# Two gated feed-forward blocks of a Trainium2 kernel: 18 of 22 gate/up pairs of each as seven block products instead of eight

## What is computed

```python
def second_block(x, ..., norm2_g, w_gate, w_up, w_down, final_g):
    for l in range(2):
        ...
        h = rms_norm(x, norm2_g[l])
        x = x + (jax.nn.silu(h @ w_gate[l]) * (h @ w_up[l])) @ w_down[l]
    return rms_norm(x, final_g)
```

## Time and profile before

| what | us |
|---|---|
| median of 3 runs (lowest to highest) | 2635.52 (2634.99 to 2636.14) |
| span of the profiled execution, first to last instruction | 2634.2 |
| what lies around the span: median less span | 1.3 |
| TensorE busy (share) | 2619.0 (99%) |
| VectorE busy (share) | 1418.1 (54%) |
| ScalarE busy (share) | 1010.3 (38%) |
| GpSimd busy (share) | 110.9 (4%) |
| mean granted TensorE clock | 0.998 of full speed |

### The profile page before, as it was taken

How to read it: one execution, slowest core, us unless ns; L and a number is a source line. 1 busy time by engine, 2 the same in 40 slices (tenths; PEclk the granted TensorE clock), 3 DMA queues, 4 the chain that set the end, 5 groups by cost and what they waited for, 6 DMA issues and landing times.

```text
span 2634.2 us, 33330 instructions
## 1 busy us (share of the span) xinstructions
PE 2619.0 (99%) x13877; PEld 2134.3 (81%) x13877; DVE 1418.1 (54%) x2209; ACT 1010.3 (38%) x1484; POOL 110.9 (4%) x87
## 2 busy tenths in 40 slices
...
GB/s 403 132 190 209 271 195 195 80 96 81 81 70 76 81 81 65 96 99 99 98 90 118 80 64 64 107 98 92 96 98 126 80 65 54 106 91 109 96 93 76
DMA packets 46744, 296.55 MB, mean 113 GB/s; under 512 B 5121, under 2 KB 7297, under 8 KB 17410
## 3 DMA queue, kind: packets, MB, share of 16 engines
...
q10 hardware_dynamic: 2, 0.00, 0.0%
...
## 4 chain that ended last, share of the span: by engine, by line
PE 96%; ACT 1%; DVE 1%; DMA 1%; issue 0%; SPq 0%; DVEq 0%; ACTq 0%
PE PS L565 95%; PE PS L623 1%; ACT WH L1078 0%; DMA RAW<-stream 0%; DMA AR<-stream 0%; DVE AA L1553 0%; DVE XT L1553 0%; ACT TMP L1078 0%; ACT AA L1078 0%; DVE Tb L1553 0%; ACT H1H L1078 0%; DVE WL L1553 0%; DVE AR L1576 0%; DVE SPL L1556 0%; DVE Vb L1826 0%
## 5 line engine op out<-in xcount | busy, mean ns | idle before, releaser
L565 PE MATMUL PS<-H1H,WH 128*128 128x512 f32 (+1 forms) x2144 | 826.6, 386 | 0.4 <-DVE H1L L1553 0.3
L565 PE MATMUL PS<-H1H,WL 128*128 128x512 f32 (+1 forms) x2144 | 814.5, 380 | 0.0
L565 PE MATMUL PS<-H1L,WH 128*128 128x512 f32 (+1 forms) x2144 | 814.5, 380 | 0.0
L1553 DVE TENSOR_TENSOR WL<-RAW,WH 128x1024 fp32r<-128x1024 f32 (+1 forms) x400 | 526.3, 1316 | 475.8 <-ACT WH L1078 474.4
L1078 ACT ACTIVATE WH<-RAW 128x1024 fp32r<-128x1024 f32 (+1 forms) x400 | 440.8, 1102 | 281.5 <-PE PS L565 250.7
L565 PEld LDWEIGHTS PS<-H1H,WH 128*128 128x128 f32 x2144 | 403.2, 188 | 82.7 <-issue 5.4
L565 PEld LDWEIGHTS PS<-H1L,WH 128*128 128x128 f32 x2144 | 403.4, 188 | 78.8 <-issue 4.1
L565 PEld LDWEIGHTS PS<-H1H,WL 128*128 128x128 f32 x2144 | 403.2, 188 | 76.6
L565 PE MATMUL PS<-H2Hb,WH 128*128 128x512 f32 (+1 forms) x408 | 161.1, 395 | 0.0
L565 PE MATMUL PS<-H2Lb,WH 128*128 128x512 f32 (+1 forms) x408 | 154.3, 378 | 0.0
L565 PE MATMUL PS<-H2Hb,WL 128*128 128x512 f32 (+1 forms) x408 | 154.1, 378 | 0.0
...
## 6 DMA issues: line engine op xcount, KB each, us to landing
...
```

The costliest lines, as they stand in the source:

```text
L565: return nc.tensor.matmul(out, weights, moving, start=start, stop=stop, skip_group_check=True)
L1553: return nc.vector.tensor_tensor(out, a, b, op)
```

## The change

In both feed-forwards the first four pairs (STD = 4) stay as they are; the other 18 (pairs 4 to 10 of the first half, all 11 of the second) are made otherwise. A pair is seen as the product of a 2 x 2 matrix of weight blocks (two halves of the 1024 channels, gate and up) with a 2 x 2 matrix of activation blocks (two halves of the channels, two halves of 256 tokens). Instead of eight block products there are seven, of sums of blocks: A11, S1, S2, A12, S4, A22, S3, each 4 x 3 matmuls of 256 columns, in this order on TensorE, with `prod` counting five of them and `mm` the other two (S4 and S3).

- Weights: VectorE makes the four sums S1 to S4 of a pair (512 values per partition each) into QV; ScalarE rounds A11 with A12, S1 with S2, A22, and S4 with S3 to QH (`weights_high`, `sums_high`, `second_high`, `rest_high`); VectorE subtracts to get QL (`weights_low`, `sums_low`, `second_low`, `rest_low`). QH lies where WH was, QL and QV both where WL was, and there is one of each: a part of pair s + 1 is written when the product of pair s that read the same part is done (`product`).
- Activations: during the first four pairs VectorE makes, once for each layer, seven blocks of 1024 values (`factors`: 8 products with gain and SG, 4 sums or differences, 7 low parts) and ScalarE their 7 high parts (`factors_high`). SG is folded in, so those 18 pairs need neither the product with SG on VectorE nor the one on GpSimd.
- Results: products shared by two results are copied out of PSUM by ScalarE into KEPT1 and KEPT2 in four copies of 256 columns (`kept`); VectorE then forms `SI = D - KEPT1` and `E = E + KEPT2` (D, E are the two banks), and the rest is as before, with `gated` of pair s run in the turn of pair s + 1.
- Order: the homes of the tiles in WH/WL are no longer t mod 3 from here on. In front of the second feed-forward's first seven product the eight standard tiles have homes 2, 0, 1, 2, 1, 0, 1, 2; in the first feed-forward they go on in turn (1, 2, 0, 1, 2, 0, 1, 2). The eight tiles of `w_down` between the halves have 0, 1, 2, 0, 1, 0, 1, 2. Waits of SyncE and the counts of GpSimd follow.

The core of the diff:

```diff
+STD = 4
...
+def seven(t):
+    return any(t in range(f0 + 2 * STD, f0 + 22) or t in range(f0 + 30, f0 + 52) for f0 in (FFN2, FFN3))
...
+def before(t, home):
+    return max((u for u in HOME if u < t and HOME[u] == home), default=3)
...
+        self.QH, self.QL, self.QV = at("QH", 68096, 3584, F32R), at("QL", 84992, 3584, F32R), at("QV", 84992, 3584)
...
+        self.TH, self.TL, self.TV = at("TH", 165888, 7168, F32R), at("TL", 194560, 7168, F32R), at("TV", 194560, 8192)
+        self.KEPT1, self.KEPT2 = at("KEPT1", 110592, 512), at("KEPT2", 112640, 512)
...
+    def vacant(self, t):
+        last = before(t, HOME[t])
+        run = [s for s, p in enumerate(PAIRS) if last < p < t]
+        if run and HOME[t] == 0:
+            return self.prod, 5 * run[-1] + 4
+        return self.mm, mm_at(PAIRS[run[-1]] + 1 if run else last)
...
+    def product(self, s, name):
+        t = PAIRS[s]
+        if t - 1 in HOME:
+            homes = {"A11": (0,), "S1": (0, 1), "S2": (1,), "S4": (1,), "S3": (1, 2), "A22": (2,)}[name]
+            return self.mm, max(mm_at(before(t, i)) for i in homes)
+        if name in ("S4", "S3"):
+            return self.mm, mm_at(t - 2 + (name == "S3"))
+        return self.prod, 5 * s - 5 + {"A11": 4, "S1": 2, "S2": 3, "A22": 5}[name]
...
+            def product(o, m, out, first=False):
+                for k in range(4):
+                    wh, wl = (X[:, o + 128 * k:o + 128 * k + 128] for X in (c.QH, c.QL))
+                    hi, lo = (X[:, 1024 * m + 256 * k:1024 * m + 256 * k + 256] for X in (c.TH, c.TL))
+                    mm(out, wh, hi, first and k == 0, False)
+                    mm(out, wh, lo, False, False)
+                    ins = mm(out, wl, hi, False, k == 3)
+                return ins
+            vacate(BANK[t + 1])
+            q.wait_ge(c.ql, 4 * s + 1)
+            q.wait_ge(c.tl, 7 * (f - 2) + 1)
+            product(A11, 0, E[:, 256:512], True).then_inc(c.prod, 1)
+            vacate(BANK[t])
+            q.wait_ge(c.ql, 4 * s + 2)
+            q.wait_ge(c.tl, 7 * (f - 2) + 2)
+            product(S1, 1, D[:, 256:512], True).then_inc(c.prod, 1)
+            q.wait_ge(c.kept, 4 * s + 1)
+            q.wait_ge(c.tl, 7 * (f - 2) + 3)
+            product(S2, 2, E[:, 256:512]).then_inc(c.prod, 1)
+            q.wait_ge(c.kept, 4 * s + 2)
+            q.wait_ge(c.tl, 7 * (f - 2) + 4)
+            product(A12, 3, D[:, 0:256]).then_inc(c.prod, 1)
+            q.wait_ge(c.ql, 4 * s + 4)
+            q.wait_ge(c.tl, 7 * (f - 2) + 5)
+            product(S4, 4, D[:, 256:512]).then_inc(c.mm, 1)
+            q.wait_ge(c.kept, 4 * s + 3)
+            q.wait_ge(c.tl, 7 * (f - 2) + 6)
+            product(A22, 5, E[:, 0:256]).then_inc(c.prod, 1)
+            q.wait_ge(c.tl, 7 * (f - 2) + 7)
+            product(S3, 6, E[:, 256:512]).then_inc(c.mm, 1)
+            free[BANK[t]], free[BANK[t + 1]] = freed(j, False), freed(j, True)
...
+    def weights_high(s):
+        ready, raw = c.pair(s)
+        q.wait_ge(*ready)
+        q.wait_ge(*c.product(s, "A11"))
+        act(c.QH[:, A11:A11 + 1024], raw[:, 0:1024]).then_inc(c.qh, 1)
...
+    def rest_high(s):
+        q.wait_ge(c.sum4, s + 1)
+        q.wait_ge(c.sum3, s + 1)
+        act(c.QH[:, S4:S4 + 1024], c.QV[:, S4:S4 + 1024]).then_inc(c.qh, 1)
...
+    def gated_high(f, t0, j):
+        jj = j % HC
+        q.wait_ge(c.gm, 22 * f + j + 1)
+        if j == HC:
+            q.wait_ge(c.mm, mm_at(t0 + 29))
+        act(chunk(c.GH[f], jj), c.SI[f][jj % 2][:, :]).then_inc(c.gh, 1)
...
+    def seven_kept(f, t0, j):
+        t = t0 + 30 * (j // HC) + 2 * (j % HC)
+        s, D, E, SI = PAIRS.index(t), PS[BANK[t]], PS[BANK[t + 1]], c.SI[f][j % HC % 2]
+        more = seven(t + 2)
+        q.wait_ge(c.prod, 5 * s + 1)
+        q.wait_ge(c.sa, 22 * (f - 2) + j)
+        act(c.KEPT1[:, 0:256], E[:, 256:512]).then_inc(c.kept, 1)
+        if j % HC and seven(t - 2):
+            gated_high(f, t0, j - 1)
+        q.wait_ge(c.prod, 5 * s + 2)
+        q.wait_ge(c.c2, s)
+        act(c.KEPT2[:, 256:512], D[:, 256:512], scale=-1.0).then_inc(c.kept, 1)
+        q.wait_ge(c.prod, 5 * s + 3)
+        act(c.KEPT1[:, 256:512], E[:, 256:512]).then_inc(c.kept, 1)
+        if more:
+            weights_high(s + 1)
+            sums_high(s + 1)
+        else:
+            prep(t + 2)
+        q.wait_ge(c.sa, 22 * (f - 2) + j + 1)
+        act(SI[:, :], SI[:, :], ACT.Silu).then_inc(c.si, 1)
+        if more:
+            second_high(s + 1)
+        q.wait_ge(c.mm, mm_at(t + 1))
+        act(c.KEPT2[:, 0:256], E[:, 256:512]).then_inc(c.kept, 1)
+        if more:
+            rest_high(s + 1)
+        else:
+            prep(t + 3)
+            gated_high(f, t0, j)
     def ffn(f, t0, v=None, late=None, gains=None):
...
                     act(SI[:, :], SI[:, :], ACT.Silu).then_inc(c.si, 1)
                 prep(ta + 3)
+                if follow is not None:
+                    sums_high(follow)
+                if f > 1:
+                    factors_high(f, {1: (0, 3, 4), 2: (5, 6)}.get(jj, ()))
+                if f > 1:
+                    gated_high(f, t0, j)
+                    if follow is not None:
+                        second_high(follow)
+                        rest_high(follow)
+                    continue
...
+            if f > 1 and not half:
+                second_high(PAIRS.index(t0 + 30))
+                rest_high(PAIRS.index(t0 + 30))
...
+    def more_sums(s):
+        raw = c.pair(s)[1]
+        q.wait_ge(*c.product(s, "S2"))
+        q.wait_ge(c.sum1, s + 1)
+        tt(c.QV[:, S2:S2 + 512], c.QV[:, S1:S1 + 512], raw[:, 0:512], ALU.add).then_inc(c.sum2, 1)
...
+    def third_sum(s):
+        raw = c.pair(s)[1]
+        q.wait_ge(*c.product(s, "S3"))
+        tt(c.QV[:, S3:S3 + 512], raw[:, 0:512], raw[:, 1024:1536], ALU.add).then_inc(c.sum3, 1)
+    def weights_low(s):
+        q.wait_ge(c.qh, 4 * s + 1)
+        q.wait_ge(*c.product(s, "A11"))
+        tt(c.QL[:, A11:A11 + 1024], c.pair(s)[1][:, 0:1024], c.QH[:, A11:A11 + 1024].bitcast(F32), ALU.subtract
+           ).then_inc(c.ql, 1)
...
+    def factors(f, some):
+        l, V = f - 2, [c.TV[:, 1024 * m:1024 * m + 1024] for m in range(8)]
+        spread = c.TV[:, :].rearrange("p (m k t) -> p m k t", m=8, k=4)
+        sums = {8: (1, 0, 7, ALU.subtract), 9: (2, 4, 1, ALU.add), 10: (6, 7, 4, ALU.subtract),
+                11: (5, 3, 2, ALU.subtract)}
+        for n in some:
+            if n < 8:
+                q.wait_ge(c.nrs, NORMN[5 + 2 * l] + 1)
+                out = spread[:, 0:8:7, n] if n < 4 else spread[:, 3:5, n - 4]
+                stt(out, c.xk(n).rearrange("p (h t) -> p h t", h=2), c.cols("norm2_g_2", 8 * l + n),
...
+    def gated(f, j):
+        n, SI, t = 22 * f + j + 1, c.SI[f][j % HC % 2], (FFN2, FFN3)[f - 2] + 30 * (j // HC) + 2 * (j % HC)
+        s, P = PAIRS.index(t), PS[BANK[t + 1]]
+        q.wait_ge(c.mm, mm_at(t + 1))
+        q.wait_ge(c.kept, 4 * s + 4)
+        tt(P[:, :], P[:, :], c.KEPT2[:, :], ALU.add).then_inc(c.c2, 1)
+        q.wait_ge(c.si, n)
+        q.wait_ge(c.c2, s + 1)
+        tt(SI[:, :], SI[:, :], P[:, :], ALU.mult).then_inc(c.gm, 1)
...
+    def seven_out(f, t0, j):
+        t = t0 + 30 * (j // HC) + 2 * (j % HC)
+        s, D, SI = PAIRS.index(t), PS[BANK[t]], c.SI[f][j % HC % 2]
+        more, past = seven(t + 2), j % HC and seven(t - 2)
+        third_sum(s)
+        if past:
+            gated(f, j - 1)
+        rest_low(s)
+        if past:
+            gated_low(f, j - 1)
+        if more:
+            first_sum(s + 1)
+            more_sums(s + 1)
+            weights_low(s + 1)
+        else:
+            prep(t + 2)
+        q.wait_ge(c.mm, mm_at(t))
+        q.wait_ge(c.kept, 4 * s + 3)
+        q.wait_ge(c.gl, 22 * f + j - 1 if j % HC > 1 else 0)
+        tt(SI[:, :], D[:, :], c.KEPT1[:, :], ALU.subtract).then_inc(c.sa, 1)
+        if more:
+            fourth_sum(s + 1)
+            sums_low(s + 1)
+            second_low(s + 1)
+        else:
+            prep(t + 3)
+            gated(f, j)
+            gated_low(f, j)
     def ffn(f, t0, v=None, gate=None, gains=None):
         if f < 2:
...
+                follow = PAIRS.index(ta + 2) if seven(ta + 2) else None
                 prep(ta + 2)
+                if follow is not None:
+                    weights_low(follow)
+                if f > 1:
+                    factors(f, ((), (4, 5, 6, 7), (10, 11, 12), (15, 16))[jj])
...
                 prep(ta + 3)
+                if follow is not None:
+                    first_sum(follow)
+                    more_sums(follow)
+                    fourth_sum(follow)
+                    sums_low(follow)
+                if f > 1:
+                    factors(f, ((0, 1, 2, 3), (8, 9), (13, 14), (17, 18))[jj])
...
-                    q.wait_ge(c.sp, n - 44)
+                    q.wait_ge(c.sp, STD * (f - 2) + j + 1)
...
+                if follow is not None:
+                    second_low(follow)
...
```

(46 more changed lines are left out.)

90 lines of the change are left out of this document (80 added, 10 removed).

## The result

| what | before | after | forecast |
|---|---|---|---|
| median, us (runs beside each other, 4 each) | 2635.78 | 2656.56 | 2646.6 |
| lowest to highest | 2634.99 to 2636.14 | 2655.90 to 2656.76 | 2632 to 2656 |
| span of the profiled execution | 2634.2 | 2654.6 | 2645.3 |
| mean granted clock | 0.998 | 0.995 | |

The ratio is 1.0079, with a 95% interval of 1.0064 to 1.0093: 0.8% slower, nearly twice the loss that was forecast (20.8 us instead of 11.1) and 0.6 us above the range. The span grew by 20.4 us instead of 11.1.

The account below looks back on a forecast made before the run. TensorE, 99% busy, bounds the kernel before; afterwards a ring of waits sets the pace. Work -28.8, ring +15.4, first-half entries +19.8, second-half entries +1.7, clock +3.0: total +11.1, giving 2646.6 us, range 2632 to 2656.

Parts of the forecast that it names:

- the clock: Long wait after S1 of each layer's first seven-product pair: clock falls to half, 1.5 us a layer, 3.0 in all.
- the ring: TensorE, VectorE and ScalarE waiting in turn from KEPT1's copy to the next pair's: 10.56 us a step, +15.4 over 32.
- TensorE's work: Matmul time saved over the changed pairs of both layers: -28.8 us.
- entries of the first halves: S2 of pair 4 late because factors fill VectorE's queue in pairs 0 to 3: 8.3 + 11.5 = 19.8 us.
- entries of the second halves: S2 late behind the last down tile's residual, second_low and third_sum: 0.84 us each, 1.7 in all.
- What it removes on TensorE: Each changed pair: 84 matmuls of 256 columns take 10.08 us instead of 10.88, saving 0.80.
- The rival without a ring: Neither ring nor entry binds: 2608, needing the ring's 4.2 us of VectorE to be elsewhere; chance 0.06.
- The rival in which the factors are hidden: First halves' entries cost nothing if the first third_sum starts by about 100 instead of 108.3: 2624; chance 0.08.
- all of it comes through (2608): The matmuls' whole saving reaches the time, with neither ring nor entry binding: 2608 us; chance 0.06.

Follow-up runs that it names:

- the last two experiments: Changed kernel with rest_high behind KEPT1's first copy and gated_high behind KEPT2's: 2626.01; the same plus second waits removed, second-layer homes in turn, factors ahead of low parts: 2614.24.
- the experiment on the homes: Changed kernel with two down tiles' homes swapped, so the second feed-forward's eight tiles go 1, 2, 0, 1, 2, 0, 1, 2: 2652.82, ratio 1.0065.
- five small edits of order: Changed kernel with rest_high and gated_high behind copies, two second waits removed, second-layer homes in turn, factors ahead of low parts: 2614.24, ratio 0.9919.

## Why the prediction was right in kind and too small in size

The direction, the mechanism and the places of the waits were as forecast; the clock alone fell earlier than foreseen. The range missed by 0.6 us because every term of loss was too small. The step that failed is the ring's sum: it was put at 10.56 us a step and measured 10.77, so the 32 steps lost 22.0 us and not 15.4.

| term | forecast | measured |
|---|---|---|
| TensorE's work | -28.8 | -28.8 |
| ring, 32 steps | 15.4 | 22.0 |
| entries of the first halves | 19.8 | 8.8 + 12.1 = 20.9 |
| entries of the second halves | 1.7 | 2 x 0.93 = 1.9 |
| clock | 3.0 | 2.05 + 2.31 = 4.4 |
| one longer wait (0.71 instead of 0.43, at 2376.93) | 0 | 0.3 |
| sum | 11.1 | 20.7 |

The span grew by 20.4; of the 0.3 between, 0.2 lies ahead of the change (the first `SI` at 1661.25 instead of 1661.47). Of the 10.0 by which the median is above the forecast, 9.3 is in the span, and 0.7 around it (2656.56 - 2654.6 = 2.0 instead of 1.3). The 1.3 set the median of some executions against the span of another; execution by execution what lies around the span is 1.7 to 1.9 in the kernel before and 1.9 to 2.2 in the changed one.

- **What it removes on TensorE** was right: 84 matmuls at 0.120, seven products without a gap between them, 10.08 us as soon as nothing stops them, as the last two experiments show. By the gap rule of the Trainium skill ("TensorE: Matmul & The Clock Gate", Back-to-back issue gap) it would be 109 ns a matmul; the page gives it for an isolated matmul, and these come in a stream, for which no run here shows 109.
- **The ring** was the right bound, with the right members. Moving one instruction out of it gave 24.8 us, 0.6 us of work beside it nothing. Its length is the step that failed: 10.77, not 10.56. The operations were right to 0.02. The hand-overs were not: S2 and A12 to `weights_high` 3.29 from the end of the copy instead of 0.16 + 2.88 + 0.18 = 3.22; `fourth_sum` to `sums_low` and `third_sum` to `rest_high` 0.78 each instead of 0.72. That is 0.07 + 0.06 + 0.06 of the 0.21. With the fulfilled wait in front of the blocking one taken away, two of the three fell to 0.72 and 3.23; for `sums_low`, which has such a wait too, it wasn't tried. The number of waits alone doesn't explain it: the row from which the forecast took its 0.72 (OC to OSL) stands behind two waits as well, there the blocking one first and the fulfilled one behind it. Whether a change of their order would have done is open. 32 x 0.21 = 6.7 us, two thirds of the error. The range's upper end had room for that, but not for 1.4 of clock, 1.1 of entries and 0.7 outside the span on top of it. That the listed wait ahead of S2, 0.43, looks like the forecast's 0.48 is luck: what a step loses is 0.69. The rival without a ring says that 4.2 us of VectorE would have to be elsewhere; by the forecast's own sum the six operations on the ring take 4.94, and 4.2 is what lies beside it.
- **The first halves' entries** were right within 0.5 and 0.6 us, by following the queue: `third_sum` at 1708.5 (forecast 1708.3). The home of f0 + 4 cost 3.3 more (forecast 3.2), and the experiment on the homes gave 3.7 back.
- **The second halves' entries** were right (0.93 against 0.84). The down tiles were not delayed, and TensorE waited for no load there; ScalarE's `weights_high` did, 5.2 us in each layer (at 1830.12 in the first), 18 us ahead of the S2 that was late.
- **The clock** fell in each layer, as foreseen, but not in the place foreseen, the wait behind S1: it fell behind or in the wait ahead of S1. 1.5 a layer was too low, 2.05 and 2.31 were within its bound of 2.5. The measured loss follows from the rows: 4.7 us of matmuls 0.21 apart instead of 0.12 lose 4.7 x (1 - 0.12 / 0.21) = 2.0, and nothing of it was given back by the ring. The Trainium skill states ("TensorE: Matmul & The Clock Gate", HAM oscillation) that a burst after an idle gap starts at half rate. The trace agrees for S2 in both layers and for S1 in the second, behind 5.55 us; S1 of the first layer, behind 3.12 us, still started at 0.12 a matmul.
- **The rival in which the factors are hidden** remains false as the kernel stood, and moving them gave half: their cover was partly GpSimd's. That all of it comes through (2608) was false as well, but five small edits of order came within 6 us of it.
